# A one-core decoder trunk with expert retrieval: two norms applied to scores in place of rows, fewer pair sums, joined maps, shorter roots, narrower bias loads, new stops

## The chip, the cores and the metric

The kernel runs on one core of a Trainium2 chip. The metric is the device time of one execution, in microseconds. TensorE does matrix products and transposes, VectorE and ScalarE element-wise work, GpSimd issues the indirect gathers, and SyncE issues the plain loads and stores; all transfers run on the core's 16 DMA engines. The engines have separate instruction queues, each executed in order, and meet at semaphores.

## The reference, cut to what matters

```python
h = rmsnorm(x, norm_mix);   x = x + hybrid_mixer(h, ...)      # 4 MLA heads | RG-LRU | 4 differential heads, then W_out
h = rmsnorm(x, norm_cross); x = x + memory_cross_attention(h, rmsnorm(mem, norm_mem), ...)
h = rmsnorm(x, norm_ffn);   x = x + peer_ffn(h, ...)
return rmsnorm(x, norm_final)

def rmsnorm(x, g): return x * rsqrt(mean(x * x) + EPS) * g
# differential head, per query row:  w = softmax(s_0 + bias) - lam * softmax(s_1 + bias);  o = rmsnorm(w @ v)
# cross attention:  p = softmax(q k / sqrt(256));  o = p v
# PEER, per token and head (8 heads, 128 keys on each side, 16384 experts):
top_s, top_i = top_k(q . keys, 16)                       # for both halves of the query
cand = top_s[0][:, None] + top_s[1][None, :]             # 16 x 16 sums
best_s, best_c = top_k(cand, 16)                         # ia = best_c // 16, ib = best_c % 16
experts = top_i[0][ia] * 128 + top_i[1][ib];  g = softmax(best_s)
y = sum_k g_k * gelu(x . u[experts_k]) * v[experts_k]    # rows of 1024 f32 from two tables in HBM
```

The sequence has 1024 tokens of width 1024, the memory 256 rows, all in f32. With 8 heads of 16 experts, each token needs 128 rows of `u` and 128 of `v`.

## The kernel before, in words

The 1024 tokens are worked in 8 blocks of 128 (one token to a partition). A block has a *front* (norms, projections, LRU, attention, cross attention, choice of experts) and a *retrieval* of 128 positions. At position p, GpSimd gathers one `u` row and one `v` row per token (2 x 512 KB), VectorE multiplies the `u` row with the token's `h_cur` (`multiply_row`, L1794), ScalarE makes a diagonal matrix of a coefficient (L1300), and TensorE adds the `v` row to the sum (`add_row`, L1046; 13 positions later). Each eighth `v` row is added by VectorE (L1815). Both rings have 8 slots.

The front of block b+1 is worked beside the retrieval of block b. Its order is written out by hand: `PIECES` lists the stages with weights, and in the loops the tables `TENSOR_STOPS`, `VECTOR_STOPS` and `SCALAR_STOPS` give, for each `pace.part(...)` of a stage, the position up to which the engine first works off the retrieval. Nothing is scheduled at run time: an engine that waits inside the front holds back the rows that stand behind it in its queue, and so their ring slots.

Block 0 has no retrieval beside it. Its front, here the *opening*, runs from the start to 321 us; the only work interleaved is that on the memory's keys and values (`mem_piece`, 32 pieces on TensorE, placed by `MEM_AT`, one piece per position from 24 on). A piece uses one 256 KB weight slice of the ring `w_ring` (7 slots), which SyncE loads in order with all its other transfers. The opening also computes the next block's norm and projection (`next_norm`, `next_0` to `next_4`).

What the change touches:

- The two middle norms (`norm_cross`, `norm_ffn`). The product before them (`row_product`, L965) makes 1024 columns in two halves, VectorE adds each half to `x_next` (L1663), ScalarE squares and sums the row (L1094), VectorE computes 1/sqrt by integer estimate and three Newton steps (`root_x`, `rsqrt`, L1356 to L1361, 12 operations on one column), scales the row (L1492), TensorE transposes it in 8 tiles (L814), and VectorE applies the gain on the way from PSUM (`gain_x`, L1514). Then the query product starts (`queries`, `col_tile`, L823).
- A differential head (`diff`): two score products, masked maximum (L1599), exponentials (L1213), then the map e0/sum0 + e1*(factor/sum1) in two passes (L1631, L1632).
- The choice of experts (`choose`, for 4 heads at a time): 1024 pair sums (L1714), top 16 of 256 for each head (`top16`: MAX8, FIND_INDEX8, MATCH_REPLACE8), index arithmetic and two one-hot lookups.
- Each bias load (L520) brings 128 x 1024 f32, whatever number of keys the block sees (`key_tiles`: 2 tiles of 128 for blocks 0 and 1, 4 for 2 and 3, 6 for 4 and 5, 8 for 6 and 7).

## Time and profile before

| | us |
|---|---|
| median of 3 runs (lowest, highest) | 3621.62 (3620.49, 3624.6) |
| the profiled execution | 3622.51 |
| its span in the trace | 3620.3 |
| TensorE busy (83% of the span) | 3001.4 |
| VectorE busy (67%) | 2434.2 |
| GpSimd busy (63%) | 2285.0 |
| ScalarE busy (23%) | 822.6 |
| moved by DMA | 1332.85 MB |

The span is the time between the first and the last recorded instruction; the profiled execution's own time is 2.2 us longer. A line number is that of the kernel before; a helper's line stands for all that call it. In a window row the DMA share is the mean busy share of the 16 DMA engines and can read slightly over 1. A matmul with f32 operands counts twice in the trace's counts (x128 for 64 matmuls), a transpose once (x8 for 8).

### The profile page before, as it was taken

To read this page: it belongs to the slowest core of one execution; us is meant where nothing else is said; L and a number is where in the kernel's file an instruction comes from. 1 tells how busy PE (TensorE), PEld (TensorE's weight loads), DVE (VectorE), ACT (ScalarE), POOL (GpSimd) and SP (SyncE) were. 2 spreads that over 40 slices of the span, in tenths; PEclk is the share of its full clock that TensorE was granted. 3 is DMA by queue.
4 is the path that set the end of the run, shared out by engine and by line. 5 is a ranking of instruction groups with operands and counts; after the bars stand their busy time and mean duration, and the time that the engine had idled before them with its cause. 6 is when DMAs were issued, how large, how long until landed. Compare 5 with 4: busy or idle time off the path is not lost.

```text
span 3620.3 us, 38076 instructions
## 1 busy us (share of the span) xinstructions
PE 3001.4 (83%) x11032; PEld 1680.5 (46%) x11032; DVE 2434.2 (67%) x5948; ACT 822.6 (23%) x1924; POOL 2285.0 (63%) x2085
## 2 busy tenths in 40 slices
PE   7876798878987889878998799878998789976667
PEld 6465355534554345544555355544455445522222
DVE  6229655876577864887568775777657876596554
ACT  3111321123211322114211231113321142211111
POOL 1004765777666766767656775666666676577776
PEclk9987899989999999999999899999999999998999
DMA  7447999999999999999999999999999999999998
GB/s 258 144 140 264 386 394 404 402 385 386 390 399 405 352 388 403 405 389 375 383 399 401 369 370 393 402 405 346 358 403 396 399 359 350 400 362 398 409 409 349
DMA packets 425169, 1332.85 MB, mean 368 GB/s; under 512 B 47616, under 2 KB 48768, under 8 KB 424320
## 3 DMA queue, kind: packets, MB, share of 16 engines
q0 software_dynamic: 294912, 1073.87, 76.4%
q1 hardware_dynamic: 128896, 252.28, 19.2%
q10 hardware_dynamic: 1152, 4.19, 0.3%
...
q14 instruction: 113, 0.93, 0.1%
...
## 4 chain that ended last, share of the span: by engine, by line
PE 38%; DMA 23%; POOL 18%; DVE 11%; issue 8%; ACT 1%; SPq 0%; DVEq 0%; ACTq 0%; POOLq 0%
PE ps_sum L1046 19%; DMA rows<-in_peer_u,ids_u 13%; POOL rows L651 9%; POOL rows L641 9%; DMA w_ring<-in_wstream 7%; PE ps_p L823 5%; PE ps_s L965 4%; DMA rows<-in_peer_v,ids_u 2%; PE ps_p L915 1%; DVE rows L1794 1%; PE ps_s L907 1%; DVE feat_b L1693 1%; PE ps_s L903 1%; PE ps_p L999 1%; PE ps_t L889 1%
## 5 line engine op out<-in xcount | busy, mean ns | idle before, releaser
L1046 PE MATMUL ps_sum<-rows,diag 128*128 128x512 f32 x3584 | 1737.3, 626 | 289.3 <-DMA rows<-in_peer_v,ids_v 138.1
L1794 DVE CUSTOM_DVE_ANT_0 rows<-rows,h_cur 128x1024 f32<-128x1024 f32 x1024 | 1233.6, 1223 | 635.3 <-DMA rows<-in_peer_u,ids_u 611.4
L641 POOL DMA_INDIRECT rows<-in_peer_u,ids_u x1024 | 1138.4, 1112 | 698.1 <-issue 545.9
L1046 PEld LDWEIGHTS ps_sum<-rows,diag 128*128 128x128 f32 x3584 | 673.6, 199 | 1174.4 <-issue 1018.1
L651 POOL DMA_INDIRECT rows<-in_peer_v,ids_v x512 | 551.9, 1078 | 368.7 <-PE ps_sum L1046 229.8
L651 POOL DMA_INDIRECT rows<-in_peer_v,ids_u x512 | 579.9, 1133 | 217.6 <-issue 130.5
L1300 ACT ACTIVATE diag<-ident,acts 128x128 f32<-128x128 f32 x896 | 330.2, 395 | 1064.1 <-PE ps_sum L1046 783.1
L823 PE MATMUL ps_p<-hT,w_ring 128*128 128x128 f32 x3968 | 500.6, 284 | 54.7 <-DMA w_ring<-in_wstream 48.1
L823 PEld LDWEIGHTS ps_p<-hT,w_ring 128*128 128x128 f32 x3968 | 482.2, 198 | 117.9 <-DMA w_ring<-in_wstream 63.6
L1599 DVE CUSTOM_DVE_ANT_0 e<-ps_s,bias_t 128x256 f32<-128x256 f32 (+3 forms) x96 | 78.9, 822 | 149.9 <-PE ps_s L903 81.3
L1815 DVE SCALAR_TENSOR_TENSOR x_cur<-rows,acts,x_cur 128x1024 f32<-128x1024 f32 x128 | 164.4, 1284 | 13.6 <-DMA rows<-in_peer_v,ids_v 13.6
L1213 ACT ACTIVATE e<-e,small 128x256 f32<-128x256 f32 (+3 forms) x96 | 79.4, 827 | 253.5 <-DVE small L1601 253.3
L965 PE MATMUL ps_s<-w_ring,hT 128*128 128x512 f32 x256 | 120.9, 624 | 17.9 <-DMA w_ring<-in_wstream 10.8
L1288 ACT ACTIVATE acts<-dots 128x8 f32<-128x8 f32 x128 | 26.5, 207 | 477.7 <-DVE dots L1794 477.2
L965 PE MATMUL ps_s<-w_ring,feat_b 128*128 128x512 f32 x256 | 119.2, 601 | 17.5 <-DMA w_ring<-in_wstream 16.8
L1663 DVE TENSOR_TENSOR x_next<-x_next,ps_s 128x512 f32<-128x512 f32 x32 | 22.0, 687 | 155.0 <-PE ps_s L965 155.0
L1693 DVE FIND_INDEX8 feat_b<-feat_b,e 128x8 uint32<-128x128 f32 (+1 forms) x384 | 122.5, 329 | 0.0
L907 PE MATMUL ps_s<-k_diff,feat_a 32*128 32x512 f32 (+1 forms) x192 | 89.5, 573 | 31.2 <-DVE small L1601 31.2
L1689 DVE MAX8 feat_b<-e 128x8 f32<-128x128 f32 (+1 forms) x384 | 97.4, 323 | 3.5 <-DVE small L1361 0.2
L1087 ACT ACTIVATE feat_a<-ps_p 128x512 f32<-128x512 f32 (+2 forms) x48 | 25.9, 539 | 281.2 <-PE ps_p L823 281.2
L965 PEld LDWEIGHTS ps_s<-w_ring,hT 128*128 128x128 f32 x256 | 48.9, 198 | 85.3 <-issue 54.4
L965 PEld LDWEIGHTS ps_s<-w_ring,feat_b 128*128 128x128 f32 x256 | 46.8, 190 | 85.8 <-issue 48.9
...
## 6 DMA issues: line engine op xcount, KB each, us to landing
...
bias_t<-bias_rows SPq DMA_DIRECT2D x40, 512.0 KB, 6.8
rows<-in_peer_u,ids_u POOLq DMA_INDIRECT x1024, 7.9
rows<-in_peer_v,ids_u POOLq DMA_INDIRECT x512, 6.6
rows<-in_peer_v,ids_v POOLq DMA_INDIRECT x512, 14.3
...
bias_t<-in_x SPq DMA_DIRECT2D x8, 512.0 KB, 5.2
out<-x_cur ACTq DMA_DIRECT2D x8, 512.0 KB, 5.7
```

The source lines that it names most:

```text
L641: pool.indirect_dma_start(u_rows[:, j % G_RING, :], None, peer_u, bass.IndirectOffsetOnAxis(ap=ids_u[:, j:j + 1], axis=0)).then_inc(u_land ...
L651: pool.indirect_dma_start(v_rows[:, j % G_RING, :], None, peer_v, bass.IndirectOffsetOnAxis(ap=ids[:, j:j + 1], axis=0)).then_inc(v_landed ...
L823: ins = pe.matmul(dst, w[:, k, :], hT[:, kt, :], start=(kt == 0), stop=(kt == KT - 1))
L907: ins = pe.matmul(ps_s[:, c0:c1], q_diff[r:r + DK, half // 4, :], k_diff[r:r + DK, half // 4, c0:c1], start=True, stop=True)
L965: pe.matmul(ps_s[:, n * 512:(n + 1) * 512], lhs[:, kt, :], w, start=(kt == 0), stop=(kt == KT - 1)).then_inc(w_used, 1)
L1046: ins = pe.matmul(ps_sum[:, c * 512:(c + 1) * 512], diag[:, n % 4, :], v_rows[:, j % G_RING, c * 512:(c + 1) * 512], start=(n == 0), stop= ...
L1213: act.activation(buf[:, 0:keys_n], buf[:, 0:keys_n], ACT.Exp, bias=small[:, 32 + n:33 + n], accum_out=small[:, 48 + n:49 + n]).then_inc(s_ ...
L1300: act.activation(diag[:, n % 4, :], ident[:, :], ACT.Copy, scale=coef[:, j:j + 1]).then_inc(diag_made, 1)
L1689: dve.max(v[:, first:first + 8], s).then_inc(top_step, 1)
L1693: dve.max_index(i[:, first:first + 8], v[:, first:first + 8], s).then_inc(top_step, 1)
L1794: dve.tensor_tensor_reduce(row, row, h_cur[:, :], 1.0, 0.0, ALU.mult, ALU.add, dots[:, p:p + 1]).then_inc(u_used, 1)
L1815: dve.scalar_tensor_tensor(x_cur[:, :], v_rows[:, j % G_RING, :], coef[:, j:j + 1], x_cur[:, :], ALU.mult, ALU.add)\
```

## The change

It has seven parts.

1. *Norms.* The rows that go into the two query products are no longer scaled by the root: TensorE transposes `x_next` itself, half by half (`turn_added`), the first half inside the row product, after 12 of its 16 slices. The gain is applied as before, for `norm_cross` into `pT` in place of `hT`. The root is computed afterwards and enters as a scale on the scores: in the exponential of the cross attention (`small[:, 5:6]`), and in the copy of the key scores out of PSUM (`small[:, 105:106]`, with a new semaphore `rooted`). `h_cur` takes the root in the same operation as the gain.
2. *Roots.* `rsqrt_mean` has 9 operations on one column where `tensor_scalar` and `rsqrt` had 12 (three norms per block and the final one).
3. *Pair sums.* The 16 largest of 16 x 16 sorted sums all lie in the first 4 rows or the first 4 columns: 4 x 16 + 12 x 4 = 112 sums per head are built in two operations, the top 16 is taken of 112, and the place is turned back into two indices by five more operations on 64 elements.
4. *Maps.* A differential head computes e0 + e1*(factor*sum0/sum1) in one pass; the division by sum0 comes in `join`, on the head's output.
5. *Bias loads.* They bring only the columns of the block's keys (at least as many for the mask that is loaded a block ahead).
6. *Memory pieces.* `MEM_AT` becomes a list: 4 pieces at position 24, 4 at 26, 3 at 28, 2 at 29, and one each from 31 to 49.
7. *Stops.* All three tables have new numbers.

```diff
-    "diff_2": (45, 46, 49, 50), "diff_3": (50, 52, 52, 53), "join": (55, 57), "mix_out": (57, 57, 57, 57, 57),
+    "diff_2": (44, 47, 47, 49), "diff_3": (49, 51, 52, 53), "join": (53, 57), "mix_out": (58, 58, 58, 58, 58),
...
-MEM_AT = 24
+MEM_AT = [24] * 4 + [26] * 4 + [28] * 3 + [29] * 2 + list(range(31, 50))
...
-                sp.dma_start(bias_t[:, turn % 2, :], bias_rows[h, bass.ds(at, P), bass.ds(left, SEQ)]).then_inc(bias_landed[turn % 2], 16)
+                keys_n = P * (key_tiles(b) if turn else mask_tiles[0])
+                sp.dma_start(bias_t[:, turn % 2, 0:keys_n], bias_rows[h, bass.ds(at, P), bass.ds(left, keys_n)])\
+                  .then_inc(bias_landed[turn % 2], 16)
...
+            for first, last, wide[0] in LOOPS:
+                mask_tiles[0] = max(n for f, _, n in LOOPS if f <= last)
...
+            def turn_half(src, g):
+                for k in range(4):
+                    ins = pe.transpose(ps_t[g][:, k * P:(k + 1) * P], src[:, (4 * g + k) * P:(4 * g + k + 1) * P], ident[:, :])
+                ins.then_inc(turned, 1)
...
+            def turn_added(b, n, g):
+                pe.wait_ge(out_added, 4 * b + 2 * (n - 1) + g + 1)
+                turn_half(x_next, g)
...
+                        if n == 1 and kt == 4:
+                            turn_added(b, norm, 0)
                         w = block_slice(b, first + n * KT + kt)
                         pe.matmul(ps_s[:, n * 512:(n + 1) * 512], lhs[:, kt, :], w, start=(kt == 0), stop=(kt == KT - 1)).then_inc(w_used, 1)
...
-                                         bias=small[:, 64 + h:65 + h], accum_out=small[:, 68 + h:69 + h])
+                                         bias=small[:, 64 + h:65 + h], scale=small[:, 5:6], accum_out=small[:, 68 + h:69 + h])
...
+            def rsqrt_mean(y, total, h, t, step=run):
+                step(dve.tensor_scalar(h, total, 0.5 / D, 0.5 * EPS, ALU.mult, ALU.add))
+                step(dve.tensor_scalar(t.bitcast(I32), h.bitcast(I32), 1, None, ALU.logical_shift_right))
+                step(dve.tensor_scalar(y.bitcast(I32), t.bitcast(I32), -1.0, float(0x5F3759DF - 0x400000 - 2 ** 31), ALU.mult, ALU.add))
+                for _ in range(3):
+                    step(dve.scalar_tensor_tensor(t, y, h, y, ALU.mult, ALU.mult))
+                    step(dve.scalar_tensor_tensor(y, t, 1.5, y, ALU.subtract, ALU.mult))
...
+            def norm(b, n):
+                pace.part(0.3)
+                gain_x(b, n, 1)
+                root_x(b, n, (5, 105)[n - 1])
+                if n == 2:
+                    dve.nop().then_inc(rooted, 1)
...
-                run(dve.tensor_scalar(e1[:, 0:keys_n], e1[:, 0:keys_n], small[:, 74:75], None, ALU.mult))
-                dve.scalar_tensor_tensor(e0[:, 0:keys_n], e0[:, 0:keys_n], small[:, 72:73], e1[:, 0:keys_n], ALU.mult, ALU.add)\
+                dve.scalar_tensor_tensor(e0[:, 0:keys_n], e1[:, 0:keys_n], small[:, 74:75], e0[:, 0:keys_n], ALU.mult, ALU.add)\
...
-            def add_out(b, first):
+            def add_out(b, first, norm):
                 for n in range(2):
+                    if n:
+                        pace.part(0.9)
+                        gain_x(b, norm, 0)
                     pace.part((n + 1) / 2)
...
-                dve.tensor_tensor(pairs, bc(tv[:, hs, 0, :].unsqueeze(3), wide_shape), bc(tv[:, hs, 1, :].unsqueeze(2), wide_shape),
-                                  ALU.add).then_inc(top_step, 1)
+                for i0, i1, n in ((0, NEAR, TOPK), (NEAR, TOPK, NEAR)):
+                    at, shape = NEAR * i0 * (TOPK // NEAR), [P, 4, i1 - i0, n]
+                    dve.tensor_tensor(sums[:, :, at:at + (i1 - i0) * n].rearrange("p h (i j) -> p h i j", j=n),
+                                      bc(tv[:, hs, 0, i0:i1].unsqueeze(3), shape), bc(tv[:, hs, 1, 0:n].unsqueeze(2), shape),
+                                      ALU.add).then_inc(top_step, 1)
...
+                run(dve.scalar_tensor_tensor(pick[:, 0, c4], pick[:, 1, c4], float(NEAR - TOPK), pick[:, 0, c4], ALU.add, ALU.max))
+                run(dve.tensor_scalar(pick[:, 1, c4], pick[:, 0, c4], float(NEAR), float(NEAR * (TOPK - NEAR)), ALU.mult, ALU.add))
+                run(dve.scalar_tensor_tensor(pick[:, 1, c4], pick[:, 0, c4], float(TOPK), pick[:, 1, c4], ALU.mult, ALU.min))
+                run(dve.tensor_tensor(pick[:, 1, c4], pick[:, 2, c4], pick[:, 1, c4], ALU.subtract))
...
-                dve.tensor_tensor(h_cur[:, :], xs[:, :], ffn_row[:, :], ALU.mult).then_inc(handed, 1)
+                dve.scalar_tensor_tensor(h_cur[:, :], x_next[:, :], small[:, 105:106], ffn_row[:, :], ALU.mult, ALU.mult)\
+                   .then_inc(handed, 1)
```

How instructions stand on TensorE in the opening, between the up-projection of the keys and values and the first values product (L792 are pieces of the memory's keys, 4 matmuls a piece; L874 the gates, L881 the sum for the LRU's norm, L903 the scores, L889 transposes, L915 the values). Before:

```order
L865 MATMUL ps_t<-wukv,feat_a 128x256
L792 MATMUL ps_sum<-rows,w_ring 128x256 x4
L874 MATMUL ps_t<-e,wgate 128x128 x8
L792 MATMUL ps_sum<-rows,w_ring 128x256 x16
L881 MATMUL ps_t<-e,ones 128x128 x4
L792 MATMUL ps_sum<-rows,w_ring 128x256 x4
L903 MATMUL ps_s<-k_mla,feat_b 128x256 x2
```

And with the change (lines are those of the changed kernel; L803 are the pieces, L894 the gates, L901 the sum, L923 the scores):

```order
L885 MATMUL ps_t<-wukv,feat_a 128x256
L803 MATMUL ps_sum<-rows,w_ring 128x256 x16
L894 MATMUL ps_t<-e,wgate 128x128 x8
L803 MATMUL ps_sum<-rows,w_ring 128x256 x28
L901 MATMUL ps_t<-e,ones 128x128 x4
L803 MATMUL ps_sum<-rows,w_ring 128x256 x8
L923 MATMUL ps_s<-k_mla,feat_b 128x256 x2
```

Four pieces instead of one stand ahead of the gates, seven instead of four ahead of the LRU's sum and two instead of one behind it: 13 of 32 pieces ahead of the first scores, where 6 stood.

VectorE beside the output product in the first loop (block 1; L1663 adds a half, L1514 applies the gain, L1794 multiplies a row with `h_cur` and stands as two entries; `small` holds the root). Before:

```order
L1663 TENSOR_TENSOR x_next<-x_next,ps_s 128x512 x2
L1480 TENSOR_SCALAR small<-small 128x1
L1356 TENSOR_SCALAR small<-small 128x1
L1357 TENSOR_SCALAR small<-small 128x1
...
L1361 SCALAR_TENSOR_TENSOR small<-small 128x1
L1492 TENSOR_SCALAR xs<-x_next,small 128x1024
L1514 TENSOR_TENSOR hT<-ps_t,cols 128x512 x2
```

And with the change (L1707 adds a half, L1544 applies the gain, L1850 multiplies a row):

```order
L1707 TENSOR_TENSOR x_next<-x_next,ps_s 128x512
L1850 ISA rows,dots<-rows,h_cur 128x1024
L1850 ISA dots 128x1
L1544 TENSOR_TENSOR pT<-ps_t,cols 128x512
L1850 ISA rows,dots<-rows,h_cur 128x1024
L1850 ISA dots 128x1
L1707 TENSOR_TENSOR x_next<-x_next,ps_s 128x512
L1544 TENSOR_TENSOR pT<-ps_t,cols 128x512
L1850 ISA rows,dots<-rows,h_cur 128x1024
```

The two adds are apart, each followed by its own gain, with one row multiplied between each two of them, and the root (now L1396 to L1401) stands some rows further on.

## Rows read from the trace of the kernel before

**Rows 1.** Page: the span; GB/s in 40 equal slices.
```profile
span 3620.3 us, 38076 instructions
...
GB/s 258 144 140 264 386 394 404 402 385 386 390 399 405 352 388 403 405 389 375 383 399 401 369 370 393 402 405 346 358 403 396 399 359 350 400 362 398 409 409 349
```

**Rows 2.** Windows, four stretches: us, busy us per engine, PEclk, DMA share, GB/s.
```profile
0.00:321.20 321.20, 246.34 (x1316) 193.81 (x1316) 150.92 (x540) 58.05 (x135) 22.53 (x45) 0.89 0.59 195
321.20:3268.20 2947.00, 2507.88 (x9232) 1396.44 (x9232) 2092.24 (x5086) 715.25 (x1648) 2006.81 (x1785) 0.94 1.00 384
3330.00:3404.00 74.00, 50.43 (x100) 17.80 (x98) 40.36 (x64) 9.68 (x29) 56.55 (x58) 0.95 1.03 409
2508.00:2520.00 12.00, 10.86 (x47) 6.38 (x46) 7.95 (x14) 2.71 (x5) 5.43 (x5) 0.90 0.64 230
```

**Rows 3.** Timeline, VectorE, first middle norm: start, us, line, operation [idle before].
```profile
173.75 0.69 DVE L1663 TENSOR_TENSOR x_next<-x_next,ps_s 128x512 f32<-128x512 f32 x1 [6.18 <-PE ps_s L965]
175.65 0.15 DVE L1480 TENSOR_SCALAR small<-small 128x1 f32<-128x1 f32 x1 [1.21 <-ACT xs L1094]
...
177.96 0.75 DVE L1492 TENSOR_SCALAR xs<-x_next,small 128x1024 f32<-128x1024 f32 x1
179.65 0.69 DVE L1514 TENSOR_TENSOR hT<-ps_t,cols 128x512 f32<-128x512 f32 x1 [0.94 <-PE ps_t L814]
```

**Rows 4.** Timeline, TensorE: transposes and the two query products.
```profile
178.76 1.70 PE L814 MATMUL ps_t<-ident,xs 128*128 128x128 f32 x8 [5.05 <-DVE xs L1492]
181.25 16.78 PE L823 MATMUL ps_p<-hT,w_ring 128*128 128x128 f32 x128 [0.78 <-DVE hT L1514]
...
237.85 17.46 PE L823 MATMUL ps_p<-hT,w_ring 128*128 128x128 f32 x128 [0.78 <-DVE hT L1514]
```

**Rows 5.** Windows, two stretches of the first query product.
```profile
181.00:185.00 4.00, 3.75 (x17) 3.76 (x18) 0.19 (x1) 0.00 (x0) 0.00 (x0) 0.50 0.08 25
190.00:198.00 8.00, 8.00 (x72) 7.83 (x71) 0.00 (x0) 0.60 (x1) 0.00 (x0) 1.00 0.86 276
```

**Rows 6.** Timeline, TensorE: memory pieces around the gates.
```profile
58.78 1.89 PE L792 MATMUL ps_sum<-rows,w_ring 128*128 128x256 f32 x8
...
67.75 8.13 PE L792 MATMUL ps_sum<-rows,w_ring 128*128 128x256 f32 x32
78.49 1.16 PE L881 MATMUL ps_t<-e,ones 128*128 128x128 f32 x8 [2.61 <-DVE e L1582]
```

**Rows 7.** Timeline, SyncE: issues behind the curve stores.
```profile
73.92 2.43 SPq L448 DMA_DIRECT2D w_ring<-in_wstream  x5
```

**Rows 8.** Lines, shapes apart, choice of experts: busy us, mean ns | idle.
```profile
L1689 DVE MAX8 feat_b<-e 128x8 f32<-128x128 f32 x256 | 52.5, 278 | 1.3 <-DVE small L1361 0.2
...
L1689 DVE MAX8 feat_b<-e 128x8 f32<-128x256 f32 x128 | 44.9, 413 | 2.2
...
L1693 DVE FIND_INDEX8 feat_b<-feat_b,e 128x8 uint32<-128x256 f32 x128 | 52.4, 418 | 0.0
...
L1714 DVE TENSOR_TENSOR e<-feat_b 128x1024 f32<-128x1024 f32 x16 | 19.6, 1222 | 0.2 <-issue 0.2
...
L1738 DVE SCALAR_TENSOR_TENSOR pT<-pT 128x64 uint32<-128x64 f32 x16 | 3.6, 225 | 0.5
```

**Rows 9.** Timeline, TensorE's projection end; VectorE's gate sum.
```profile
312.98 2.17 PE L842 MATMUL ps_p<-w_ring,hT 128*128 128x128 f32 x16 [0.23 <-DMA w_ring<-in_wstream]
...
320.22 0.29 DVE L1743 TENSOR_REDUCE small<-pT 128x8 f32<-128x128 f32 x1
```

**Rows 10.** Lines, shapes apart: the multiply over e1.
```profile
L1631 DVE TENSOR_SCALAR e<-e,small 128x1024 f32<-128x1024 f32 x8 | 6.2, 771 | 0.3
...
L1631 DVE TENSOR_SCALAR e<-e,small 128x256 f32<-128x256 f32 x8 | 3.4, 429 | 0.3
```

**Rows 11.** Page, DMA issues: KB each, us to landing.
```profile
bias_t<-bias_rows SPq DMA_DIRECT2D x40, 512.0 KB, 6.8
```

**Rows 12.** Waits: us in total, times, longest us.
```profile
DVE x_next L1663 <- PE ps_s L965: 155.0, 25, 16.0
```

220 lines of the change are left out of this document (116 added, 104 removed), and 3 rows, old and new, of the table VECTOR_STOPS.

## The prediction

> **What bounds the kernel now.** I read the page's slices first, then the busy time in stretches, then the order of time on VectorE and TensorE up to 321 us. The slices [rows 1] fall in two parts. The first four carry 140 to 264 GB/s; from the fifth on they hold 346 to 409. The stretches say it sharper [rows 2]: the opening, 321.2 us, keeps the DMA engines busy for 0.59 of the time at 195 GB/s, while the 2947 us behind it have a DMA share of 1.00 at 384 GB/s, and a stretch of the last retrieval, with no front beside it, runs at 409. So there are two kernels to judge. In the opening nothing is saturated: a chain through VectorE, TensorE and ScalarE sets its length, and a microsecond cut from that chain moves everything behind it. Behind it bytes set the time, except for dips. One is in the rows: 230 GB/s and a share of 0.64 at 2508 us, in the attention of a wide block. Against 403 GB/s, the rate of the good slices, the 2947 us hold 2947 x (1 - 384/403) = 139 us of dips. The change touches the opening's chain, the bytes, and (through its stops) the dips.
>
> **The change part by part.** All durations are of the profiled execution, 3622.5 us (span 3620.3), 0.9 above the median of the runs; the sum is made against 3622.5.
>
> *Two norms in the opening.* Before, the second add starts at 173.75 and ends at 174.44; ScalarE's square gives 175.65; twelve root operations lead to 177.96; the scale of the row takes 0.75; eight transposes start at 178.76; two gains follow; the product starts at 181.25 [rows 3, 4]. That is 6.8 us from the add to the product, and about as much at the second norm, whose product starts at 237.85. With the change, square, root and scale are off this path: behind the second add come four transposes (half of 1.70 us, 0.85) and one gain (0.69), and while the gain runs TensorE already does the first four matmuls on the half turned earlier. The product then starts about 0.9 us after the add. I save 5.9 us, and pay 0.85 for the four transposes that now stand inside the row product, where TensorE has no gap: net 5.0 each, 10 us for two. The root now has the whole query product, 16 us and more, to finish in before the scores need it; that covers it nine times over. The bounds: 8 us, if the mid-product transposes also wait, to 12.
>
> *The clock behind them.* The first product ran its first 4 us at a granted 0.50, which is the 1.2 GHz level, and later at 1.00 (2.4 GHz); before it TensorE had been idle for 5.05 us but for the transposes [rows 4, 5]. At full clock 72 counts take 8.00 us, so 128 take 14.2. The two products took 16.78 and 17.46: 5.8 us over. The gap ahead of them shrinks from 5 us to under 1, so I expect most of it back: 5 us, bounds 0 (the clock falls all the same, or weights arrive late: they came at 276 GB/s at full clock, against the 404 and more that the queues carry later) and 5.8.
>
> *Memory pieces.* A piece holds TensorE for 1.9 to 2.0 us (1.89 for one, 8.13 for four) [rows 6], about 1.75 at full clock. Seven more stand ahead of the first scores. There is room: between 60.7 and 67.75 TensorE has only the gates' eight matmuls, and it waits 2.61 us ahead of the LRU's sum. But the ring holds seven slices, and the eighth is issued only at 73.92, behind the curve stores and two bias loads in SyncE's queue [rows 7]. Pieces eight to eleven, which stand ahead of the sum, so run from about 76.6 (landing some 2.7 us after issue, an estimate) to 83.6, where the sum started at 78.49. What is late next is the LRU's sum, by 5 us, and behind it the root, the first masked maximum and the scores. Seven pieces fewer behind them give 7 x 1.75 = 12.2 us back, less some 3 us in the last two heads, where no piece is left to fill TensorE's gaps. Net gain 4 us; bounds -3 (the gaps are not filled, the delay is) and +9 (no delay).
>
> *Choice of experts.* All of it is in a VectorE chain of the opening. MAX8 costs 278 ns at 128 elements and 413 at 256, so about 261 at 112; FIND_INDEX8 and MATCH_REPLACE8 differ alike (418 at 256) [rows 8]. Twenty such operations in a choice save 20 x 0.15 = 3.0 us. The 1024 sums cost 1222 ns; 256 and 192 elements cost, on the line through 225 ns at 64 elements and 1222 at 1024, about 0.42 and 0.36: 0.45 saved. The index arithmetic adds five operations on 64 elements at 0.225, 1.1 us. Net 2.35 for each choice, 4.7 for both. At the end there is a cap: VectorE first uses the gates at 320.22, and the exponential it needs stands on ScalarE behind the copy of the last projection, which TensorE ends at 312.98 + 2.17 = 315.15 [rows 9]; with the copy and the exponential that is some 315.8 (an estimate), against 315.5. I count 4.4, bounds 2.5 and 5.5.
>
> For five added operations the Trainium skill ("VectorE: DVE Perf Modes", section "The TRN2 errata") has a table row of 58 + FD cycles at 0.96 GHz, an estimate of 127 ns for 64 elements. The trace has 225 [rows 8], so the measurement decides; by the page's row the two choices would gain 1.0 us more.
>
> *Small edits in the opening.* The next block's root is three operations of 0.19 shorter, but the first key scores, which the chain also needs, stand on ScalarE behind the same square: I count 0.3. The join has two maps fewer, 0.3. In a head the multiply over e1 (0.43 at 256 elements, 0.77 at 1024 [rows 10]) goes; in the opening pieces cover it but for the last heads: 0.8. The final root is on the tail: 0.6. Together 2, bounds 1 and 3.5.
>
> *Narrower bias loads.* Each of the 40 loads brought 512 KB [rows 11]. In the blocks behind the opening the heads' loads lose 768 columns in block 1, 512 in 2 and 3, 256 in 4 and 5, times four: 9216; the masks 512, 256 and 256: 1024. 10240 columns x 512 B = 5.24 MB, at 403 GB/s 13 us. Part of these loads lies in the dips, where bytes are not the limit, so I take 10; bounds 4 and 13. Another 2.4 MB go in the opening, where they cost nothing.
>
> On what a byte costs, the Trainium skill ("DMA: Bandwidth & Descriptors", section "Where 436 GB/s comes from") says that for HBM to SBUF the HBM side binds at about 358 GB/s for a core. This case's trace shows 409 [rows 2], so the rule does not hold here; by it the same bytes would be worth 14.6 us.
>
> *VectorE's relief behind the opening.* The multiply over e1 took 0.43 to 0.77 us in four heads of seven blocks, 18 us in all, and stood where the dips are. I count a third, 6; bounds 0 and 18. Roots, norms and choices get shorter there too, some 8 us a block, but beside a DMA share of 1.0, which hides them: nothing.
>
> *Stops.* In the attention stages they move by one to three positions, both ways. I have no row for what that is worth and take 0, bounds -15 and +35, a quarter of the 139.
>
> Sum: 10 + 5 + 4 + 4.4 + 2 + 10 + 6 = 41.4 us, 25 of it in the opening. 3622.5 - 41.4 = 3581; less the 0.9 by which the profiled execution stood over the median, 3580.
>
> **The rivals.** (A) *Only the opening gains.* For it: the dips are waits of engines on one another, and the bias loads lie among them. Against it: the share of 1.00 over 2947 us. It gives 3622 - 25 - 3 = 3594. (B) *The stops close dips.* For it: 139 us are there to win, and every table is redone; a block's excess grows with its width, which is where e1's multiply was longest. Against it: the positions in the attention hardly move. With 35 us more than my sum, 3545. (C) *Slower: VectorE blocks in the output products.* Before, VectorE waited 155.0 us in 25 waits for their halves, 16.0 at the longest [rows 12]. Now it must also wait there for the transposes of each half, with one row between two waits. The u ring covers eight rows, 8 x 421/128 = 26 us, with 421 us the mean block (2947/7). As long as a wait with its neighbours stays under that, the gathers go on; beyond it each microsecond counts in 14 norms. To eat 41 us and 8 more it takes 3.5 us over in each, 29 us of blocking where 16 are seen: 3630. For it: in the new order two gains and two adds stand within three rows. Against it: the slices with these products show no dip before, with 10 us in hand. (D) *The pieces do not fit*: the LRU's sum is late by more than the 12 us given back, so that part costs 3 in place of giving 4, and the clock gives nothing: 3592; I put it with A.
>
> **How the numbers follow.** My forecast 0.50, with its own range 3562 to 3600; A with D 0.26; B 0.18; C 0.06. Three runs of before span 4 us, so what lies within 0.2%, 7 us, cannot be told from no change. A gain under 7 us needs C's mechanism in part, or both bounds of the opening at once: same 0.03. Slower 0.04, faster 0.93. The range reaches from B's middle, 3543, to 3607, where the opening gives 15 and the rest nothing; it leaves out C and the far half of B.
>
> **What would show it.** The opening, which ends with the `h_cur` operation at 321.2, should end at 297 (293 to 306). There, each query product should start within 1.2 us of the second add and take under 15 us; the LRU's sum should start 5 us later than at 78.49, and yet the last map of the differential heads be made 4 us earlier than before; a choice should be 2.3 us shorter. Behind it the bytes should fall to 1325 MB and the mean block from 421 us to about 419, the narrow blocks most. The forecast is wrong if the mean block stays at 421 (A), falls under 417 (B), or if GpSimd begins to wait for VectorE's dots while the output products run (C).

## The result, and the profile after

The changed kernel took 3573.25 us (median of 4, 3565.91 to 3591.02) beside 3621.05 for the kernel before: ratio 0.9871, 95% interval 0.9852 to 0.9890, so 47.8 us were gained where 41.4 were predicted. The sum came out near, but not by its own terms, as the stretches show. First the page of the changed kernel (its profiled execution, 3591.02 us, was the longest of the four; it answers to [rows 1, 11]), then its windows, with the columns of [rows 2].

```profile
span 3589.0 us, 37810 instructions
...
GB/s 268 129 163 305 375 403 397 404 376 376 403 403 398 364 380 403 401 390 352 402 398 403 373 394 403 400 397 369 380 403 404 397 358 384 383 376 384 365 376 330
...
bias_t<-bias_rows SPq DMA_DIRECT2D x11, 512.0 KB, 7.0
```

```profile
0.00:299.20 299.20, 236.50 (x1316) 184.77 (x1316) 141.31 (x533) 58.59 (x135) 22.57 (x45) 0.92 0.60 201
299.20:3207.80 2908.60, 2490.29 (x9232) 1397.00 (x9232) 2021.56 (x5036) 717.67 (x1648) 2010.95 (x1781) 0.94 1.01 387
3330.00:3404.00 74.00, 50.83 (x94) 18.48 (x92) 35.55 (x59) 8.48 (x25) 58.46 (x52) 0.89 0.98 364
```

In this pair of traces the opening is 22.0 us shorter, the seven blocks behind it 38.4 (2947.0 to 2908.6), and the last retrieval, whose code did not change but for the final root, is 29.1 us *longer* (352.1 to 381.2): its stretch at 3330 runs at 364 GB/s where it ran at 409. The page shows it at a glance: its last four slices fell from 398, 409, 409 and 349 to 384, 365, 376 and 330. The profiled execution stands 17.8 us over the median of the four, so not every execution need have lost these 29 us.

In the opening, VectorE at the first middle norm reads as follows (the answer to [rows 3]).

```profile
171.38 0.69 DVE L1707 TENSOR_TENSOR x_next<-x_next,ps_s 128x512 f32<-128x512 f32 x1 [2.74 <-PE ps_s L989]
172.81 0.69 DVE L1544 TENSOR_TENSOR pT<-ps_t,cols 128x512 f32<-128x512 f32 x1 [0.75 <-PE ps_t L820]
173.42 0.14 DVE L1396 TENSOR_SCALAR small<-small 128x1 f32<-128x1 f32 x1
```

The root now starts at 173.42, behind the gain, where nobody waits for it. TensorE at the same norm and the next (the answer to [rows 4]), and the granted clock in two stretches of that product (to [rows 5]):

```profile
172.12 0.65 PE L820 MATMUL ps_t<-ident,x_next 128*128 128x128 f32 x4 [0.78 <-DVE x_next L1707]
172.62 14.61 PE L843 MATMUL ps_p<-pT,w_ring 128*128 128x128 f32 x128
...
221.54 14.61 PE L843 MATMUL ps_p<-hT,w_ring 128*128 128x128 f32 x128
```

```profile
173.00:177.00 4.00, 4.00 (x37) 3.92 (x36) 2.01 (x10) 0.26 (x2) 0.00 (x0) 1.00 0.77 245
177.00:185.00 8.00, 8.00 (x74) 8.00 (x73) 0.00 (x0) 0.60 (x1) 0.00 (x0) 1.00 0.89 278
```

The product starts 0.55 us after the end of the second add (6.81 before) and runs at 1.00, the 2.4 GHz level, from its start: 14.61 us for each product in place of 16.78 and 17.46. The pieces (the answer to [rows 6, 7]; TensorE, then SyncE's queue):

```profile
56.68 7.07 PE L803 MATMUL ps_sum<-rows,w_ring 128*128 128x256 f32 x32
63.59 1.95 PE L894 MATMUL ps_t<-e,wgate 128*128 128x128 f32 x16
65.37 5.34 PE L803 MATMUL ps_sum<-rows,w_ring 128*128 128x256 f32 x24
75.68 9.42 PE L803 MATMUL ps_sum<-rows,w_ring 128*128 128x256 f32 x32 [4.96 <-DMA w_ring<-in_wstream]
84.94 1.05 PE L901 MATMUL ps_t<-e,ones 128*128 128x128 f32 x8
```

```profile
71.21 1.09 SPq L528 DMA_DIRECT2D bias_t<-bias_rows  x2
72.35 3.35 SPq L455 DMA_DIRECT2D w_ring<-in_wstream  x7
```

Seven pieces run, then TensorE waits 4.96 us for the eighth slice (issued at 72.35), and the LRU's sum starts at 84.94. The four pieces behind the wait take 9.42 us, at a granted clock of 0.50 (the 1.2 GHz level) up to 80 us; in e8, below, whose wait is 2.34 us, the same four take 7.17 at 1.00. Last, the choice of experts and the end of the opening (lines with the shapes apart, the answer to [rows 8]; then VectorE in order of time, to [rows 9]):

```profile
L1733 DVE MAX8 feat_b<-e 128x8 f32<-128x112 f32 x128 | 25.7, 262 | 3.0
...
L1763 DVE TENSOR_TENSOR e<-feat_b 128x256 f32<-128x256 f32 x16 | 6.6, 414 | 0.0
L1763 DVE TENSOR_TENSOR e<-feat_b 128x192 f32<-128x192 f32 x16 | 5.6, 348 | 0.0
```

```profile
298.17 0.29 DVE L1798 TENSOR_REDUCE small<-pT 128x8 f32<-128x128 f32 x1 [2.21 <-ACT pT L1297]
...
299.17 1.28 DVE L1814 SCALAR_TENSOR_TENSOR h_cur<-x_next,small,ffn_row 128x1024 f32<-128x1024 f32 x1
```

In order of time, the first choice (from the start of the cast ahead of its sums, at 253.82, to the start of its last index operation, at 269.25) takes 15.43 us where it took 17.84: 2.4 saved, as the prediction had it (2.35).

### The profile page after: what moved, and what is told of

Read it like the earlier page. It is cut to its first block, busy times and chain, and to the rows that moved or that the text cites. A ratio compares the mean times of both kernels' runs of the same rounds, so it can differ in the third digit from the quotient of the medians.

```text
span 3589.0 us, 37810 instructions
## 1 busy us (share of the span) xinstructions
PE 2989.5 (83%) x11032; PEld 1678.8 (47%) x11032; DVE 2353.7 (66%) x5884; ACT 825.6 (23%) x1924; POOL 2316.5 (65%) x2085
## 4 chain that ended last, share of the span: by engine, by line
PE 47%; DMA 24%; POOL 12%; DVE 9%; issue 6%; ACT 2%; SPq 0%; DVEq 0%; ACTq 0%
PE ps_sum L1074 26%; DMA w_ring<-in_wstream 8%; DMA rows<-in_peer_v,ids_v 8%; PE ps_p L843 8%; POOL rows L662 6%; POOL rows L652 6%; DMA rows<-in_peer_u,ids_u 5%; PE ps_s L989 4%; DMA rows<-in_peer_v,ids_u 3%; DVE rows L1850 2%; PE ps_s L927 1%; PE ps_p L935 1%; PE ps_p L1028 1%; PE ps_s L1013 1%; PE ps_sum L810 1%
## 5 line engine op out<-in xcount | busy, mean ns | idle before, releaser
L1074 PE MATMUL ps_sum<-rows,diag 128*128 128x512 f32 x3584 | 1764.5, 638 | 300.0 <-DMA rows<-in_peer_v,ids_v 148.1
L1850 DVE CUSTOM_DVE_ANT_0 rows<-rows,h_cur 128x1024 f32<-128x1024 f32 x1024 | 1231.5, 1223 | 556.6 <-DMA rows<-in_peer_u,ids_u 532.4
L1074 PEld LDWEIGHTS ps_sum<-rows,diag 128*128 128x128 f32 x3584 | 695.2, 204 | 1200.7 <-issue 1054.4
L662 POOL DMA_INDIRECT rows<-in_peer_v,ids_v x512 | 561.2, 1096 | 347.8 <-PE ps_sum L1074 218.3
L662 POOL DMA_INDIRECT rows<-in_peer_v,ids_u x512 | 595.4, 1163 | 183.0 <-issue 128.3
L843 PE MATMUL ps_p<-hT,w_ring 128*128 128x128 f32 x2944 | 376.6, 284 | 61.9 <-DMA w_ring<-in_wstream 58.8
L843 PEld LDWEIGHTS ps_p<-hT,w_ring 128*128 128x128 f32 x2944 | 357.5, 197 | 109.6 <-DMA w_ring<-in_wstream 69.3
L989 PE MATMUL ps_s<-w_ring,hT 128*128 128x512 f32 x256 | 121.6, 616 | 18.6 <-DMA w_ring<-in_wstream 17.8
L843 PEld LDWEIGHTS ps_p<-pT,w_ring 128*128 128x128 f32 x1024 | 119.0, 192 | 13.8 <-issue 10.2
L843 PE MATMUL ps_p<-pT,w_ring 128*128 128x128 f32 x1024 | 121.1, 276 | 2.3 <-DMA w_ring<-in_wstream 2.3
L1707 DVE TENSOR_TENSOR x_next<-x_next,ps_s 128x512 f32<-128x512 f32 x32 | 22.0, 688 | 136.5 <-PE ps_s L989 136.4
L1737 DVE FIND_INDEX8 feat_b<-feat_b,e 128x8 uint32<-128x128 f32 (+1 forms) x384 | 103.4, 279 | 0.0
L989 PEld LDWEIGHTS ps_s<-w_ring,hT 128*128 128x128 f32 x256 | 47.3, 195 | 85.7 <-issue 42.8
L1115 ACT ACTIVATE pT<-ps_t 128x128 f32<-128x128 f32 (+3 forms) x144 | 57.8, 449 | 118.0 <-PE ps_t L909 80.3
## 6 DMA issues: line engine op xcount, KB each, us to landing
rows<-in_peer_v,ids_v POOLq DMA_INDIRECT x512, 10.6
```

Of the source, the lines that this page charges most:

```text
L662: pool.indirect_dma_start(v_rows[:, j % G_RING, :], None, peer_v, bass.IndirectOffsetOnAxis(ap=ids[:, j:j + 1], axis=0)).then_inc(v_landed ...
L843: ins = pe.matmul(dst, w[:, k, :], lhs[:, kt, :], start=(kt == 0), stop=(kt == KT - 1))
L989: pe.matmul(ps_s[:, n * 512:(n + 1) * 512], lhs[:, kt, :], w, start=(kt == 0), stop=(kt == KT - 1)).then_inc(w_used, 1)
L1074: ins = pe.matmul(ps_sum[:, c * 512:(c + 1) * 512], diag[:, n % 4, :], v_rows[:, j % G_RING, c * 512:(c + 1) * 512], start=(n == 0), stop= ...
L1737: dve.max_index(i[:, first:first + 8], v[:, first:first + 8], s).then_inc(top_step, 1)
L1850: dve.tensor_tensor_reduce(row, row, h_cur[:, :], 1.0, 0.0, ALU.mult, ALU.add, dots[:, p:p + 1]).then_inc(u_used, 1)
```

## The experiments

Twelve kernels ran in four sets. The first set (e1 to e4) fell on a chip where the kernel before takes 3773 us, all others on two chips where it takes 3623 to 3628. The `h_cur` operations of a trace cut its span into the opening, the fronts of blocks 1 to 5, those of 6 and 7, and the last retrieval. All in us; "set" is the median of the kernel before in the same set.

| kernel | opening | blocks 1-5 | 6-7 | last | median | set | ratio (95%) |
|---|---|---|---|---|---|---|---|
| before, profiled | 321.2 | 2099.9 | 847.1 | 352.1 | 3621.6 | | |
| changed, profiled | 299.2 | 2080.6 | 828.0 | 381.2 | 3573.3 | 3621.1 | 0.9871 (0.9852 to 0.9890) |
| e5 before | 317.8 | 2098.9 | 845.2 | 352.6 | 3629.2 | 3623.0 | 1.0013 (0.9996 to 1.0030) |
| e6 changed | 302.8 | 2085.0 | 824.8 | 354.5 | 3575.4 | 3623.0 | 0.9859 (0.9826 to 0.9892) |
| e7 stops of before | 302.2 | 2105.7 | 846.9 | 354.2 | 3622.1 | 3623.0 | 0.9994 (0.9971 to 1.0016) |
| e8 more matmuls | 299.2 | 2083.3 | 832.5 | 376.2 | 3575.9 | 3623.0 | 0.9846 (0.9809 to 0.9882) |
| e9 before, new stops | 321.6 | 2162.8 | 867.5 | 354.1 | 3705.8 | 3625.4 | 1.0213 (1.0184 to 1.0242) |
| e10 opening | 295.1 | 2071.8 | 828.4 | 360.0 | 3566.0 | 3625.4 | 0.9841 (0.9814 to 0.9868) |
| e11 bias and maps | 307.0 | 2086.4 | 834.0 | 366.8 | 3581.5 | 3628.1 | 0.9870 (0.9841 to 0.9899) |
| e12 half the stops | 305.1 | 2097.5 | 840.0 | 357.2 | 3606.7 | 3628.1 | 0.9944 (0.9927 to 0.9962) |
| e1 changed | 304.9 | 2207.3 | 870.7 | 379.9 | 3779.6 | 3773.3 | 1.0030 (1.0007 to 1.0053) |
| e2 stops of before | 302.9 | 2215.0 | 884.9 | 380.3 | 3769.1 | 3773.3 | 1.0003 (0.9977 to 1.0029) |
| e3 bias full | 307.4 | 2217.6 | 875.8 | 380.6 | 3775.6 | 3773.3 | 1.0004 (0.9977 to 1.0032) |
| e4 maps apart | 304.5 | 2220.8 | 874.6 | 378.8 | 3789.3 | 3773.3 | 1.0074 (1.0035 to 1.0114) |

On the chips where the kernel before takes 3623, equal code scatters by 6 us in the opening (299.2 to 305.1 in the five kernels with the changed one's opening), by 13 in blocks 1 to 5 (2071.8 to 2085.0) and by 8 in blocks 6 and 7 (824.8 to 832.5), with four kernels each (the changed one, e6, e8 and e10); over the seven blocks it is 15.6 (2900.2 to 2915.8). A term smaller than that isn't settled by one trace. The stretches are those of one profiled execution each, which lay up to 17.8 us from the median of its kernel, so a stretch and a median are compared with care.

### First set: another chip

The yardstick, e1:

> The changed kernel unchanged, as the yardstick of this set: 3573 us, h_cur of the first block at about 299, seven blocks of the middle 415.5 us each. If the last retrieval has two regimes, its length (381 us in the profiled run of the changed kernel, 352 in the kernel before) is a coin of its own in each execution: 350 to 385 here. If the changed kernel lengthens it for good, it is 381 again.

e2 puts the tables of before back:

```diff
 TENSOR_STOPS = {
-    "latents": (6,), "mla_up": (10,), "gates": (20, 20), "recur": (20, 25), ...
+    "latents": (3,), "mla_up": (10,), "gates": (15, 21), "recur": (27, 27), ...
```

> The changed kernel with the stop tables of the kernel before (the entry that the shorter tables lack is added). Theory S (the new stops gave most of the 5.5 us per middle block): the middle blocks go back to 420 or more, h_cur of the first block stays within 1 us of 299, and the whole is 25 to 35 us longer than the yardstick. Theory B (fewer bytes and fewer VectorE passes gave it, stops nothing, as predicted): the middle blocks stay within 1 us of the yardstick's, the whole within 7 us. Between the two: wide blocks (5 to 7) alone slow down, by 10 us each, 30 us in all.

e3 loads the bias over all columns again:

```diff
-                sp.dma_start(bias_t[:, turn % 2, 0:keys_n], bias_rows[h, bass.ds(at, P), bass.ds(left, keys_n)])
+                sp.dma_start(bias_t[:, turn % 2, :], bias_rows[h, bass.ds(at, P), bass.ds(left, SEQ)])
```

> The changed kernel with the bias of the positions loaded over all 1024 columns again, as in the kernel before, 5.24 MB more. Bytes theory (predicted: bytes are time at 395 to 403 GB/s behind the opening, 11.6 us in the narrow blocks, 1.4 in the opening): 8 to 14 us longer, all in blocks 1 to 4, none in the wide ones, since those load all columns in both. Rival (these transfers fit in dips, where the queue is not full): 0 to 4 us.

e4 scales the second map of a differential head in a pass of its own again:

```diff
-                dve.scalar_tensor_tensor(e0[:, 0:keys_n], e1[:, 0:keys_n], small[:, 74:75], e0[:, 0:keys_n], ALU.mult, ALU.add)
+                run(dve.tensor_scalar(e1[:, 0:keys_n], e1[:, 0:keys_n], small[:, 74:75], None, ALU.mult))
+                dve.scalar_tensor_tensor(e0[:, 0:keys_n], e1[:, 0:keys_n], 1.0, e0[:, 0:keys_n], ALU.mult, ALU.add)
```

> The changed kernel with the second map of a differential head scaled in a pass of its own again, 4 passes per block up to 1024 wide (about 1.1 us each in a wide block). Relief theory (VectorE holds up retrieval rows there, so its passes are time in wide blocks): 4 to 6 us per wide block, 1 to 2 in the narrow ones, 12 to 20 us in all. Rival (VectorE has slack in the middle blocks): within 4 us, of which 0.8 in the opening.

None of the four came out in the sizes expected, since the expectations were made for the faster chips. Windows of e1, the same three parts:

```profile
0.00:304.90 304.90, 242.73 (x1316) 190.10 (x1316) 141.43 (x532) 58.60 (x135) 22.53 (x45) 0.90 0.60 198
304.90:3382.90 3078.00, 2580.19 (x9232) 1451.21 (x9232) 2014.24 (x5036) 716.98 (x1648) 2025.81 (x1785) 0.91 0.97 366
3440.00:3514.00 74.00, 49.88 (x95) 18.60 (x94) 35.89 (x59) 8.66 (x26) 53.60 (x53) 0.88 0.97 364
```

The opening is as long as on the other chips. Behind it transfers come at 366 GB/s in place of 387, and even the pure retrieval stays at 364. There the whole gain is gone: the changed kernel is 0.3% slower than before (an interval that excludes 1). By the medians it is 10 us faster with the *old* stops, e2, but the intervals of the two ratios overlap, so that the new stops lose there is not settled; that they do not gain the 47 us of the second set is. The stretches of this set can't decide it: the profiled execution of e1 was the shortest of its ten, that of e2 the longest. The full bias loads (e3) cost nothing that can be seen. The extra pass (e4) costs 9.7 us by the medians, from five executions beside ten, again with intervals that overlap. The whole set was measured on one chip at one time, so whether the chip or the hour makes the difference is open. (In the expectation of e3, as in that of e11, the blocks are misnamed: a load is narrower in blocks 1 to 5, and full only in 6 and 7. Of the 7.6 MB in e11's, 5.2 lie there, and 2.4 in the opening.)

### Second set: who gave the blocks' gain

e5 is the kernel before and e6 the changed kernel, both unchanged; e7 is the changed kernel with the tables of before, as e2.

> The kernel before, unchanged. In the first set the kernel before took 3773 us in the middle and the changed kernel 3780, where 3621 and 3573 had been measured: memory moved 352 GB/s in place of 369. If the chip itself sets this (theory M: the transfers of the retrieval come slower there, so whatever the engines save is waited for at memory), then here, where the kernel takes 3773, its opening is still 18 to 24 us longer than the changed kernel's, its middle blocks are as long as the changed kernel's within 3 us each, and its last retrieval is 380, not 352. If the gain is undone by the changed kernel's own last retrieval (theory L), that of this kernel is 352 on this chip too.

> The changed kernel unchanged, the yardstick of this set. On a chip where the kernel before takes 3621: 3573. Where it takes 3773: 3775 to 3780, as in the first set. Theory M expects the ratio to fall with the rate of memory alone.

> The changed kernel with the stop tables of the kernel before, a second time: in the first set it was 10 us faster than the changed kernel, not 25 to 35 slower, with one middle block 11 us shorter and others up to 13 longer. Theory S (stops fit one rate of the transfers): where the kernel before takes 3621 these tables cost 15 us or more, where it takes 3773 they gain 5 to 12. Theory N (stops nothing): within 5 us of the changed kernel on either.

e8 adds a matmul behind each summed row of the last retrieval, and one wait ahead of that retrieval:

```diff
                     ins.then_inc(v_used, 1)
+                    if isinstance(bp, int) and bp == NB - 1:
+                        pe.matmul(ps_s[:, 0:256], ident[:, :], keys[:, 0:256], start=True, stop=True)
...
+            pe.wait_ge(k_out, 2 * NB)
```

> The changed kernel, where in the last retrieval alone TensorE does one matmul of 256 columns more behind each summed row (112 in all, into a PSUM tile that nobody reads), so that it stands idle less between rows. Clock theory (the last retrieval takes 380 in place of 352 because TensorE falls to the lower clock between rows and then sums too late): granted clock at or near 1.00 from the first block's end of work to the end, 2.57 us per row, last retrieval 350 to 356, 24 to 30 us gained. Rival (memory sets it: the rows come at 375 GB/s whatever TensorE's clock): clock up, length 378 to 382 as before, or some us longer for the added work.

This set ran where the kernel before takes 3623, so e5's question (is its opening longer on the slow chip too?) was not answered. What it did answer is e7. The opening kept its gain to within 1 us of e6, and the seven blocks went from 2909.8 us (e6) to 2952.6, more than the kernel before needs (2944.1). The new stops are worth 43 us in these blocks, and 46.7 by the medians (3622.1 to 3575.4). The shorter norms, choices, maps and bias loads, placed at the old stops, are worth nothing there that can be seen: the blocks are 8 us longer than e5's, which is within the scatter of one trace. Windows of the front of block 6 in two parts of 105 us and the rest, first of e6, then of e7:

```profile
2387.80:2492.80 105.00, 82.55 (x252) 41.89 (x253) 84.72 (x178) 36.08 (x79) 80.24 (x63) 0.89 0.98 373
2492.80:2597.80 105.00, 100.30 (x378) 54.15 (x378) 67.62 (x144) 33.68 (x67) 71.82 (x64) 1.00 1.00 384
2597.80:2808.20 210.40, 187.61 (x810) 117.49 (x808) 142.96 (x403) 39.03 (x93) 137.66 (x131) 0.96 1.03 404
```

```profile
2407.90:2512.90 105.00, 80.67 (x227) 39.18 (x225) 78.59 (x166) 32.02 (x73) 75.52 (x61) 0.89 0.93 356
2512.90:2617.90 105.00, 100.45 (x364) 53.10 (x364) 67.72 (x144) 36.06 (x69) 67.48 (x62) 0.98 0.98 365
2617.90:2838.90 221.00, 194.28 (x853) 121.19 (x852) 149.12 (x417) 40.65 (x99) 142.54 (x135) 0.98 1.03 403
```

The operations are the same. In the first 105 us e7 moves 17 GB/s less, in the next 19; together 3.8 MB, which at 403 GB/s is 9.4 of the 10.6 us by which the block is longer. The rest of the block runs at 403 in both. So in this block nearly all of the difference is the depth of the dips in its first half, where the attention lies.

e8 did not keep the clock at 1.00 (0.87 to 0.96 in the windows below), so it tests less than it was meant to; yet it settles something, with the traces beside it. Windows of the last retrieval, of e8, of the changed kernel and of e7:

```profile
3240.00:3320.00 80.00, 62.36 (x145) 29.67 (x146) 44.66 (x79) 10.81 (x29) 62.68 (x57) 0.87 1.00 380
...
3480.00:3560.00 80.00, 66.02 (x165) 30.83 (x164) 42.99 (x71) 10.95 (x32) 60.81 (x64) 0.96 1.03 409
```

```profile
3440.00:3520.00 80.00, 57.49 (x103) 20.73 (x103) 40.46 (x65) 9.37 (x28) 62.37 (x58) 0.87 0.99 374
```

```profile
3320.00:3390.00 70.00, 52.48 (x93) 19.94 (x92) 38.84 (x62) 9.21 (x26) 53.36 (x55) 0.83 1.03 409
```

The retrieval has two paces, 364 to 380 GB/s (364 is the changed kernel's at 3330, above) and 409. e7 runs at 409 with a granted clock of 0.83, lower than the 0.87 of the slow stretches: the low clock does not cause the slow pace. e8 changes pace in the middle, at about 3480. What tips it over is not shown.

### Third set: the stops without the operations, and the opening

e9 is the kernel before, with the three tables of the changed one up to `cross_out`:

```diff
-    "latents": (3,), "mla_up": (10,), "gates": (15, 21), "recur": (27, 27), ...
+    "latents": (6,), "mla_up": (10,), "gates": (20, 20), "recur": (20, 25), ...
```

> The kernel before, with none of its operations changed, but with the changed kernel's stops in every stage up to the last output product of the cross stage (positions up to 80); from the feed-forward norm on its own stops stay, with which the order of the rest is free of a standstill. On a chip where the kernel before takes 3623 with middle blocks of 420.6: theory S1 (the new stops are better by themselves): blocks of 415 to 417, 25 to 40 us gained, opening unchanged at 318 to 321. Theory S2 (the stops only fit the changed operations; the gain needs both): blocks of 420 to 425, nothing gained or up to 20 lost. On a chip where the kernel before takes 3773, both are worth 10 us at most.

It is 80 us *slower* than the kernel before (3705.8 to 3625.4), 86 us of it in the seven blocks. Theory S1 falls. Of S2 the claim holds that the gain needs both the stops and the operations, but the loss is four times as large as it allowed. Where it lies in the front of block 6 is read from the windows of e5, then of e9 (the second 105 us and the rest):

```profile
2521.70:2626.70 105.00, 101.88 (x370) 54.01 (x369) 75.63 (x160) 33.35 (x67) 69.60 (x61) 0.97 0.98 366
2626.70:2845.10 218.40, 191.54 (x825) 118.44 (x824) 147.89 (x397) 38.89 (x95) 139.71 (x131) 0.96 1.03 398
```

```profile
2589.40:2694.40 105.00, 87.71 (x286) 46.58 (x285) 68.27 (x148) 29.93 (x58) 62.47 (x54) 0.89 0.92 343
2694.40:2924.10 229.70, 201.07 (x878) 123.58 (x877) 149.99 (x401) 41.45 (x102) 147.37 (x137) 0.98 1.01 388
```

Against 403 GB/s the second part loses 6.0 us more in e9, and the rest 5.8, which is the block's 11.3. The seam, where the old positions go on (82 of 128), lies in the rest, so up to half of the loss may be the seam's; the half ahead of it is the new stops' own. e9 with no seam was not run.

e10 has two edits in the opening:

```diff
-MEM_AT = [24] * 4 + [26] * 4 + [28] * 3 + [29] * 2 + list(range(31, 50))
+MEM_AT = [24] * 4 + [26] * 3 + [29] * 3 + list(range(30, 52))
...
-                              "project_1": lambda b: second_project(), "project_4": lambda b: first_exps()}, 0)
+                              "project_1": lambda b: second_project(), "project_4": lambda b: first_exps(),
+                              "next_4": lambda b: None, "choose_1": lambda b: (choose(b), project_4(b + 1))}, 0)
```

> The changed kernel with two edits of its opening alone, at places that the trace tells apart. First, 7 in place of 8 products of pieces stand ahead of the second part of the gates, and the later ones one to two places further apart. Second, ScalarE takes the exponentials of the gates before the copy of the last projection of the next block. Piece theory (the 5 us that the first attention stage waits for a weight behind the pieces come from the order, and go with it): the LRU sum starts 2 to 5 us earlier than 84.9, the last transposes of the heads 1 to 3 us earlier than 145.4. Rival (the pieces cost their own duration wherever they stand): the sum moves, the heads' last transposes stay within 1 us. Gates theory: the 2.2 us that VectorE waits at 298 shrink to under 1; rival: VectorE then waits for TensorE or the projection's copy delays block 1, the wait is as long. Whole: 1 to 5 us shorter than the changed kernel, under what three rounds can tell; the trace decides.

Both edits did what they were meant to, the first by more than expected: the LRU's sum starts 7.2 us earlier than 84.94 (2 to 5 were expected), the last transposes of the heads at 143.09, 2.3 us earlier than 145.38. TensorE in order of time:

```profile
57.92 7.07 PE L803 MATMUL ps_sum<-rows,w_ring 128*128 128x256 f32 x32
64.83 1.95 PE L894 MATMUL ps_t<-e,wgate 128*128 128x128 f32 x16
66.61 5.34 PE L803 MATMUL ps_sum<-rows,w_ring 128*128 128x256 f32 x24
77.75 2.08 PE L901 MATMUL ps_t<-e,ones 128*128 128x128 f32 x8 [5.79 <-DVE e L1620]
```

and VectorE at the end of the opening:

```profile
293.85 0.23 DVE L1794 SCALAR_TENSOR_TENSOR pT<-pT 128x64 uint32<-128x64 f32 x1
294.11 0.29 DVE L1799 TENSOR_REDUCE small<-pT 128x8 f32<-128x128 f32 x1
```

The LRU's sum no longer stands behind the eighth slice: it starts 19.8 us after the first piece, as before the change (19.7), and not 28.3. And the gate sum follows at once, where VectorE waited 2.21 us. The opening is 295.1 us, 6.6 under the mean of the five others (301.7). At 3566.0 us, ratio 0.9841, it is the fastest kernel measured, beside ratios of 0.9859 and 0.9871 for the changed one; those were other sets, and the intervals overlap, so that it beats the changed kernel rests on the trace, not on the times.

### Fourth set: bytes, passes, and half of the stops

e11 joins the edits of e3 and e4.

> The changed kernel with two edits undone that act in different blocks: the bias loads take all columns again (7.6 MB more, in blocks 1 to 4 alone; the wide blocks 5 to 7 load all in both), and the second map of a differential head is scaled in a pass of its own again (a VectorE pass up to 1024 wide per head, the dearest in the wide blocks). Against the yardstick's blocks of 407.4, 415.8, 420.5, 421.0, 420.2, 420.4, 404.3 on such a chip. Bytes theory: the first four grow by 11 to 18 us in sum (7.6 MB at 403 GB/s are 18.9, less where they fit in dips). Passes theory: the last three grow by 4 to 6 us each. Fit theory (the stops fit one set of operations, and any change of them costs more than its own duration): over 8 us per wide block for 4.4 us of passes. Rival to all: within 1 us per block.

e12 takes the old entries for `latents` to `join`, and the new ones behind:

> The changed kernel with the old stops in the mixing stages alone (latents to join, positions up to 57), and its own behind them. The old tables throughout cost 6.1 us per middle block (421.8 in place of 415.7). Theory F (the dips lie in the first 200 us of a block, so the gain does too): 4 to 6 us per block here, with GB/s from 26 to 210 us behind the start of a block as low as under the old tables. Theory R (the rest of the block, where norms, queries and choices are shorter, gives it): 0 to 2 us per block. Whole: 28 to 42 us more than the changed kernel's, or under 14.

In blocks 6 and 7, where only the pass differs (2 blocks x 4 heads x 0.82 us = 6.6, less 0.5, since the pass behind it takes 1.23 us in place of 1.29), e11 is 5.6 us longer than the mean of the four kernels with equal code there (828.4). In blocks 1 to 5 it is 6.2 us longer (2086.4 to 2080.2), for 11.5 us of passes and 5.2 MB, and the rate rose with the bytes, as its window beside e6's shows (e11 first):

```profile
307.00:2393.40 2086.40, 1785.32 (x6640) 1011.53 (x6640) 1444.85 (x3622) 504.10 (x1180) 1435.32 (x1274) 0.93 1.01 390
```

```profile
302.80:2387.80 2085.00, 1789.60 (x6640) 1012.88 (x6640) 1434.36 (x3602) 503.84 (x1180) 1439.99 (x1274) 0.93 1.01 387
```

Both differences are smaller than the scatter, and e11's profiled execution was 14.7 us longer than its median. By the ratios the two edits cost even less: 0.9870, beside 0.9859 and 0.9871 for the changed kernel, some 0 to 4 us, though the ratios hold the scatter of the last retrieval too. So the bytes theory fails (11 to 18 us for the bytes alone), and so does the fit theory (over 8 us per wide block). The passes theory (4 to 6 us in each wide block) is not borne out either, since blocks 6 and 7 have 2.8 each; that a pass costs at most about its own duration is what can be said. e12 is 28.9 us longer in the seven blocks than the mean of those four (2937.5 to 2908.6): two thirds of e7's 44.0. The dips are back too: the first and second 105 us of block 6 run at 358 and 367 GB/s, where e7 has 356 and 365, and e6 373 and 384. Theory F holds, at 4.1 us per block. The remaining 15 us are left for the stops behind position 57, but that is as much as equal code scatters.

## Why the prediction was right, and where it was not

The time (3573 for 3580), the sign and the bytes (1325 MB) were right. The opening was right by its mechanism, but for the memory pieces. Behind the opening the gain came from a term that had been put at 0, and that the whole was still near is luck. By the steps:

**What bounds the kernel.** The split into an opening that is a chain and blocks in which the dips decide held in every trace. What did not hold is that fewer bytes come back there as time (below). The rate of the transfers does matter: on the chip of the first set they ran at 366 GB/s, 5% less than 387, and the seven blocks took 3078.0 us, 6% more. But a few MB more or less in loads beside the gathers did not show. "The narrow blocks most" did not come either: blocks 6 and 7, which save no bias byte, gained 17.8 us in the mean (846.2 to 828.4), 8.9 each, blocks 1 to 5 gained 19.2 (2099.4 to 2080.2), 3.8 each.

**The opening.** Predicted 25 us, shown 22.0 in the two profiles, and 18.5 from the means (320.2 over three kernels with before's opening, 301.7 over five with the changed one's). Cut at the first piece, the first query product, the second, and the next norm's (which starts at 273.28 before, 253.96 after), e5 and the profile of before against those five:

- From the first piece to the first query product 122.5 before, 117.4 after: 5.1 gained. The norm alone gave 6.3 by its rows, less 0.65 for the inner transposes, so 5.6, as predicted (5.0). That leaves -0.5 in the mean (-2.6 to 1.5 in the five traces) for the *memory pieces* with the maps and the join, where 4 + 0.8 + 0.3 were counted. The last map of the heads, expected 4 us earlier, came 2.6 earlier (145.4 for 148.0 where the transposes behind it start), with 2.1 of that from an earlier first piece. This is the failed step of the opening: the sum was late not by 5 us, as stated, but by 6.5 (8.5 from the first piece), since the wait of 4.96 us for the eighth slice fell ahead of four pieces (the slice came 3.3 us after its issue, where 2.7 was estimated), and these ran in 9.42 us, at the lower clock, where the prediction had 7.0. It had named the cause, SyncE's queue, and then counted on the seven pieces fewer behind the sum to win more than the delay lost. e10, with the eighth piece behind the sum, has 112.6, that is 9.8 gained: the 10.1 of the prediction's terms together.
- From the first to the second query product 56.3 before, 49.1 after: 7.3, for 5.0 of the norm and 2.2 of the first product's clock.
- From there to the next norm's product 35.4 before, 32.6 after: 2.8, the second product's clock. Together the clock gave 5.0 of 5 predicted.
- From there to `h_cur` 47.9 before, 44.9 after: 3.0, where 4.7 were counted (choice and next root). The choices did give what was counted (2.4 and 2.5 us). The cap took more than estimated: the gates' exponential stood behind the projection's copy, and VectorE waited 2.21 us for it. With the order turned, in e10, the stretch gains 4.9.

**Bytes.** 10 us counted, bounds 4 and 13; e11 and e3 show nothing that stands out (from e11: -3.6 if the passes are taken at their 85% of blocks 6 and 7, with a scatter of 7 either way). The term failed, because a DMA share of 1.00 was read as a full queue. In these traces that share says little about the rate: it was 1.01 at 387 GB/s (e6) and at 390 (e11), 1.00 at 380 and 1.03 at 409 (e8).

**VectorE's relief.** 6 counted, bounds 0 and 18. The pass costs 9.7 us by the medians of e4, and e11 has 5.6 in blocks 6 and 7 and at most 6.2 in the others, all within the scatter; 6 may be right, but no run settles it. The two terms together, 16, were 11.8 in e11's trace and 0 to 4 by its ratio.

**Stops.** 0 counted, bounds -15 and +35. This is the step that failed by most: a term put at nothing for want of a row. e7 gives 43 to 44 us for the new tables, beyond the upper bound, and the seven blocks gained 37.0 in the mean (2945.6 to 2908.6) where the forecast had 16. The terms are not even additive: the operations alone at the old stops gain nothing (8.4 longer from e5 to e7, within the scatter), the stops alone lose 86 (e9, its seam included), both together gain 34 (e5 to e6). Which of the new operations the new stops need was not tested; e11 undid the maps and the bias loads alone, not the norms or the choices. The forecast's own sign against itself (a mean block under 417) came: 415.5. So rival (B), the stops close dips, names the mechanism behind the opening, with 0.18 of the chance where the forecast had 0.50; its 3545 us were not reached.

**The last retrieval.** Not a term at all. It took 352.1 to 354.2 us in the four kernels with the old stops behind position 82, and 354.5 to 381.2 in the six with the new (mean 366.0): some 12.7 us given back, by more time in the slow pace. Six against four, and the nearest two are 0.3 us apart; also, no experiment changed this alone, so that the late stops cause it is argued, not shown. No front stands beside this retrieval, so the tables could act on it only by the state in which it is entered. It hid the overshoot: -18.5 - 37.0 + 12.7 = -42.8, near the 41.4 predicted by luck of two errors. (The medians gained 47.8 in the first comparison and 47.7 in the second set; the 5 us between lie in how the profiled executions stand to the others.)

**Rivals.** (A) is out on the chips where the kernel before takes 3623: the blocks gained too. e7 shows what it would have been. (C), VectorE blocks in the output products, is out by the time, but its waits did come. VectorE's wait for the halves shrank from 155.0 us, and new ones for the transposes, which the gains now need there, came on top: 251.0 in all, where the halves and the transposes (L1514, 9.9) made 164.9 (both lines also serve the next block's norm). This is the answer to [rows 12], with the two lines of the gains:

```profile
DVE x_next L1707 <- PE ps_s L989: 136.4, 31, 16.1
DVE hT L1544 <- PE ps_t L820: 73.2, 13, 10.6
...
DVE pT L1544 <- PE ps_t L820: 41.4, 16, 6.4
```

GpSimd waited for the dots 151.5 us in 35 waits before and 161.9 in 37 after. The sum hides a shift: from 150 to 210 us behind the start of a block, where the mixers' output product ends, the waits of all blocks came to 59.6 us before (67.2 in e5) and 101.7 after (101.5 in e6); in the rest of the block they shrank. So the sign of (C) did come, without the loss that (C) drew from it.

(D) held by half: the pieces did not fit, the clock did come back. What no rival had is that the gain depends on the chip, or on what else set the first set apart: 48 us in the other sets, 6 lost there.
